# MLA keys squared and normalised out of PSUM, prompt queries left unnormalised until the exponential

## What is computed

```python
def rmsnorm(x, g):
    ms = jnp.mean(x32 * x32, axis=-1, keepdims=True)
    return (x32 * lax.rsqrt(ms + EPS)).astype(x.dtype) * g

def mla_keys(lat, kr, p):
    kv = (lat @ p["w_ukv"]).reshape(B, K, MLA_HEADS, MLA_NOPE + MLA_V)
    k_nope, v = kv[..., :MLA_NOPE], kv[..., MLA_NOPE:]
    k_rope = jnp.broadcast_to(kr[:, :, None, :], (B, K, MLA_HEADS, MLA_ROPE))
    k = rmsnorm(jnp.concatenate([k_nope, k_rope], axis=-1), p["g_qk_k"])
    return k, v

q = (rmsnorm(c_q, p["g_q_lora"]) @ p["w_uq"]).reshape(B, L, MLA_HEADS, MLA_QK)
q = jnp.concatenate([q[..., :MLA_NOPE], rope(q[..., MLA_NOPE:], pos)], axis=-1)
q = rmsnorm(q, p["g_qk_q"])
s = jnp.einsum('bqhd,bkhd->bhqk', q, k) * (MLA_QK ** -0.5)
w = jax.nn.softmax(jnp.where(mask, s, -jnp.inf), axis=-1)
```

## Time and profile before

| | before |
|---|---|
| median of 3 runs | 1527.66 us (1523.3 to 1532.15) |
| the profiled execution, its time | 1524.81 us |
| its span in the trace | 1523.0 us |
| PE busy | 1399.7 us (92%) |
| DVE busy | 785.7 us (52%) |
| ACT busy | 623.0 us (41%) |
| mean granted PE clock | 0.96 of full |

### The profile page before, as it was taken

One profiled execution on the slowest core, in us unless ns is written; L12 is line 12 of the kernel. 1 busy time (PEld: TensorE's weight loads), 2 busy tenths in 40 slices (PEclk: granted clock), 3 DMA queues, 4 the chain that ended last, 5 costly groups with the idle time before them and its releaser, 6 DMA issues.

```text
span 1523.0 us, 21364 instructions
## 1 busy us (share of the span) xinstructions
PE 1399.7 (92%) x8622; PEld 1135.2 (75%) x8622; DVE 785.7 (52%) x1140; ACT 623.0 (41%) x966; POOL 94.2 (6%) x80
## 2 busy tenths in 40 slices
PE   5998999999999989999479999999999999899991
PEld 5995667799999756777279847668999987567770
DVE  4336546533435347887353284464433344578763
ACT  4317634422224134565243285343222232355540
POOL 0300000000000011000203000000000000110002
PEclk9999999899999999999779999999999999899996
DMA  7223300033125457998722103000333163599955
GB/s 263 70 66 105 111 1 1 1 111 103 43 77 211 161 224 262 410 411 306 240 90 70 61 2 110 0 1 19 94 110 103 44 227 132 203 365 415 414 187 204
DMA packets 95927, 229.51 MB, mean 151 GB/s; under 512 B 14410, under 2 KB 64612, under 8 KB 82916
## 3 DMA queue, kind: packets, MB, share of 16 engines
q1 hardware_dynamic: 83252, 179.58, 32.6%
q0 software_dynamic: 7360, 29.89, 5.6%
q10 hardware_dynamic: 5232, 18.88, 3.1%
HBM read 197.69 MB, written 34.84 MB: 153 GB/s over the span
## 4 chain that ended last, share of the span: by engine, by line
PE 85%; DVE 4%; DMA 4%; ACT 3%; issue 2%; POOL 1%; ACTq 0%; POOLq 0%; SPq 0%; DVEq 0%
PE ps L763 10%; PE ps L765 10%; PE ps L764 10%; PE ps L1214 7%; PE ps L1194 3%; PE ps L1192 3%; PE ps L1193 3%; PE ps L1035 3%; PE ps L1100 2%; PE ps L789 2%; PE ps L1102 2%; PE ps L1101 2%; PE ps L791 2%; PE ps L790 2%; DMA rows_back<-xrow_d,row_of 2%
## 5 line engine op out<-in xcount | busy, mean ns | idle before, releaser
L1670 DVE TENSOR_TENSOR work<-work,ps 128x544 f32<-128x544 f32 x48 | 34.6, 721 | 211.2 <-ACT work L1525 211.2
L1525 ACT ACTIVATE work<-ps 128x544 f32<-128x544 f32 x48 | 30.0, 625 | 247.4 <-PE ps L765 247.4
L764 PE MATMUL ps<-xn_r,ksv_r 128*128 128x272 f32 x384 | 112.1, 292 | 0.0
L708 POOL DMA_INDIRECT rows_back<-xrow_d,row_of x32 | 38.1, 1192 | 1192.2 <-DVE row_of L2011 976.1
L764 PE MATMUL ps<-xn_r,work_r 128*128 128x272 f32 x384 | 110.7, 288 | 0.0
L1194 PE MATMUL ps<-ew_r,rows_tok_r 128*128 128x512 f32 x256 | 100.1, 391 | 0.0
L790 PE MATMUL ps<-wr_r,qt_ht_r 128*128 128x256 f32 (+1 forms) x320 | 93.1, 291 | 0.0
L789 PE MATMUL ps<-work_r,qt_ht_r 128*128 128x256 f32 x240 | 72.4, 302 | 14.0 <-DVE rows_lo_r L1670 7.9
L1670 DVE TENSOR_TENSOR ew_r<-ew,gu_hi_a_r 128x2048 fp32r<-128x2048 f32 x32 | 73.1, 2290 | 17.1 <-ACT gu_hi_a_r L1546 17.1
L764 PEld LDWEIGHTS ps<-xn_r,ksv_r 128*128 128x128 f32 x384 | 73.7, 192 | 0.0
L764 PEld LDWEIGHTS ps<-xn_r,work_r 128*128 128x128 f32 x384 | 72.1, 188 | 0.0
(11 more groups left out here) (348 smaller groups left out, 4066.9 us busy)
## 6 DMA issues: line engine op xcount, KB each, us to landing
wr<-in_w_in SPq DMA_DIRECT2D x68, 512.0 KB, 4.7
ew<-in_w_exp_gate SPq DMA_DIRECT2D x32, 1024.0 KB, 6.6
ew<-in_w_exp_up SPq DMA_DIRECT2D x32, 1024.0 KB, 10.2
ew<-in_w_exp_down SPq DMA_DIRECT2D x32, 1024.0 KB
wr<-in_w_out SPq DMA_DIRECT2D x16, 512.0 KB, 4.1
rows_d<-yo_a ACTq DMA_DIRECT2D x16, 512.0 KB
rows_d<-yo_b ACTq DMA_DIRECT2D x16, 512.0 KB
xres_d<-x_keep SPq DMA_DIRECT2D x2, 2048.0 KB, 7.0
```

The source lines that it names most:

```text
L764: mm(out_[h], w_hi, x_lo[:, c], start=False, stop=False, skip_group_check=True)
L1670: return v_.tensor_tensor(o_, a, b, op)
```

## The change

- **Keys.** ACT no longer copies the key part to SBUF; it squares the 512 key columns straight out of PSUM. DVE adds 64 squares a head (not 96), copies the values, and writes the normalised tile with two multiplications, one of the rotated key by the factor (256 columns) and one of the key part out of PSUM (512). The copies L1414 and L1793, the 768-column square and the 768-column multiplication of a key tile are gone. The rotated key's own sum of squares is made once a layer by three DVE operations ahead of the stage (`kr_ss`, `kr_bias`), and comes in as the bias of the logarithm.
- **Queries.** The sample tile is now first (`Q_ORDER`), and is normalised as before. The four prompt tiles are not multiplied: their sums go to `q_rs`, which one logarithm and one exponential turn into factors after `softplus_tail(1)`. In the scores, the exponential takes the factor as its scale, and a new DVE operation multiplies the negated maximum (128x1) by it, behind the maximum itself. ACT now squares a query out of PSUM right after its copy.
- **Banks and order.** Products use three pairs of banks (0 to 5) and run three tiles ahead for n up to 9; all transposes use banks 6-7, so transposes(n) wait for `kq_evac(n-1)`. `busy(4, 2)` is gone.

```diff
+Q_ORDER = [4, 0, 1, 2, 3]
...
+        kr_ss, kr_bias = small[:, 72:79], small[:, 80:87]
+        q_rs = small[:, 96:128].rearrange("p (t h) -> p t h", t=4)
...
-                    b = 2 * (n % 2)
-                    if n >= 2:
-                        pe.wait_ge(kq_raw[0], at(kq_raw, l, n - 1))
+                    b = 2 * (n % 3)
+                    if 3 <= n < 10:
+                        pe.wait_ge(kq_n[0], at(kq_n, l, n - 2))
+                    if n >= 10:
+                        pe.wait_ge(kq_sq[0], at(kq_sq, l, n - 2))
...
-                kq_products(0)
-                kq_products(1)
+                for n in range(3):
+                    kq_products(n)
                 for n in range(12):
-                    if n < 10:
-                        kq_products(n + 2)
-                    m = KM[n] if n < 7 else TM[n - 7]
+                    if 7 <= n < 9:
+                        kq_products(n + 3)
+                    m = KM[n] if n < 7 else TM[Q_ORDER[n - 7]]
                     if n == 11:
-                        pe.wait_ge(kq_raw[0], at(kq_raw, l, 12))
+                        pe.wait_ge(kq_sq[0], at(kq_sq, l, 12))
                         z_products(0)
-                    if n >= 2:
-                        pe.wait_ge(kq_ev[0], at(kq_ev, l, n - 1))
-                    if n == 10:
-                        busy(4, 2)
-                    pe.wait_ge(kq_n[0], at(kq_n, l, n + 1))
+                    if n:
+                        pe.wait_ge(kq_ev[0], at(kq_ev, l, n))
+                    if n < 8:
+                        pe.wait_ge(kq_n[0], at(kq_n, l, n + 1))
+                    else:
+                        pe.wait_ge(kq_raw[0], at(kq_raw, l, n - 6))
                     if m < P:
                         stand(pe)
                     for h in range(HEADS):
-                        ins = nc.tensor.transpose(bank(4 + 2 * (n % 2) + h // 4, m, QK, P * (h % 4)),
+                        ins = nc.tensor.transpose(bank(6 + h // 4, m, QK, P * (h % 4)),
                                                   kw[0:m, n % 3, QK * h:QK * h + QK], ident[0:m, 0:m])
                     ins.then_inc(kq_tp[0], 1)
+                    if n < 7:
+                        kq_products(n + 3)
...
-                    f(kss[0:m, n % 2], kss[0:m, n % 2], ACT.Ln, bias=eps[0:m], scale=1.0 / QK).then_inc(kq_ln[0], 1)
+                    f(kss[0:m, n % 2], kss[0:m, n % 2], ACT.Ln, bias=kr_bias[0:m, n:n + 1] if n < 7 else eps[0:m], scale=1.0 / QK).then_inc(kq_ln[0], 1)
...
+                    b = 2 * (n % 3)
                     act.wait_ge(kq_mm[0], at(kq_mm, l, n + 1))
-                    if n >= 3:
+                    if n >= 2:
+                        act.wait_ge(kq_ss[0], at(kq_ss, l, n - 1))
+                    if n < 7:
+                        f(sq[0:m, n % 2, 0:HEADS * NOPE].rearrange("p (h n) -> p h n", h=HEADS),
+                          ps[0:m, b:b + 2, :].rearrange("p b (h n) -> p (b h) n", h=4)[:, :, 0:NOPE], ACT.Square).then_inc(kq_sq[0], 1)
+                        if n >= 2:
+                            kq_evac(n - 2)
+                        kq_rstd(n)
+                    else:
                         act.wait_ge(kq_tp[0], at(kq_tp, l, n - 2))
-                    if n < 7:
-                        f(kw[0:m, n % 3, :].rearrange("p (h n) -> p h n", h=HEADS)[:, :, 0:NOPE],
-                          ps[0:m, b:b + 2, :].rearrange("p b (h n) -> p (b h) n", h=4)[:, :, 0:NOPE], ACT.Copy).then_inc(kq_cp[0], 1)
-                    else:
                         f(kw[0:m, n % 3, :].rearrange("p (b n) -> p b n", b=2), ps[0:m, b:b + 2, 0:384], ACT.Copy).then_inc(kq_cp[0], 1)
-                    if n:
-                        kq_rstd(n - 1)
-                    if n >= 2:
+                        f(sq[0:m, n % 2, :].rearrange("p (b n) -> p b n", b=2), ps[0:m, b:b + 2, 0:384], ACT.Square).then_inc(kq_sq[0], 1)
+                        if n == 8:
+                            kq_rstd(7)
                         kq_evac(n - 2)
-                    act.wait_ge(kq_raw[0], at(kq_raw, l, n + 1))
...
+                act.wait_ge(kq_ss[0], at(kq_ss, l, 12))
+                f(q_rs, q_rs, ACT.Ln, bias=eps, scale=1.0 / QK).then_inc(kq_ln[0], 1)
+                act.wait_ge(kq_ln[0], at(kq_ln, l, 9))
+                f(q_rs, q_rs, ACT.Exp, scale=-0.5).then_inc(kq_rs[0], 1)
...
-                    f(pr[0:m, n % 3, 0:nk], ps[0:m, n % 3, 0:nk], ACT.Exp, bias=nmax[0:m, n % 3:n % 3 + 1],
+                    f(pr[0:m, n % 3, 0:nk], ps[0:m, n % 3, 0:nk], ACT.Exp, bias=nmax[0:m, n % 3:n % 3 + 1], scale=q_rs[:, t, h:h + 1] if t < 4 else 1.0,
...
+                kr_sq = rope_t.rearrange("p a n -> p (a n)")[:, 0:NKT * ROPE].rearrange("p (t n) -> p t n", t=NKT)
+                link(tt(kr_sq, krt[:, :, :], krt[:, :, :], ALU.mult))
+                link(v_.tensor_reduce(kr_ss, kr_sq, AX, ALU.add))
+                link(v_.tensor_scalar(kr_bias, kr_ss, 1.0 / QK, EPS, ALU.mult, ALU.add))
...
-                        v_.tensor_copy(vv[0:m, n, :].rearrange("p (h n) -> p h n", h=HEADS),
-                                       ps[0:m, b:b + 2, :].rearrange("p b (h n) -> p (b h) n", h=4)[:, :, NOPE:P])
-                        v_.tensor_copy(k3[0:m, :, NOPE:QK], krt[0:m, n, :].unsqueeze(1).to_broadcast([m, HEADS, ROPE])).then_inc(kq_raw[0], 1)
+                        rs = kss[0:m, n % 2].unsqueeze(2)
+                        kv = ps[0:m, b:b + 2, :].rearrange("p b (h n) -> p (b h) n", h=4)
+                        dve.wait_ge(kq_sq[0], at(kq_sq, l, n + 1))
+                        v_.tensor_reduce(kss[0:m, n % 2], sq[0:m, n % 2, 0:HEADS * NOPE].rearrange("p (h n) -> p h n", h=HEADS), AX, ALU.add).then_inc(kq_ss[0], 1)
+                        v_.tensor_copy(vv[0:m, n, :].rearrange("p (h n) -> p h n", h=HEADS), kv[:, :, NOPE:P])
+                        dve.wait_ge(kq_rs[0], at(kq_rs, l, n + 1))
+                        if n >= 3:
+                            dve.wait_ge(kq_tp[0], at(kq_tp, l, n - 2))
+                        tt(k3[0:m, :, NOPE:QK], krt[0:m, n, :].unsqueeze(1).to_broadcast([m, HEADS, ROPE]), rs.to_broadcast([m, HEADS, ROPE]), ALU.mult)
+                        tt(k3[0:m, :, 0:NOPE], kv[:, :, 0:NOPE], rs.to_broadcast([m, HEADS, NOPE]), ALU.mult).then_inc(kq_n[0], 1)
                     else:
...
-                    if n:
-                        kq_scale(n - 1)
-                    dve.wait_ge(kq_sq[0], at(kq_sq, l, n + 1))
-                    v_.tensor_reduce(kss[0:m, n % 2], sq[0:m, n % 2, :].rearrange("p (h n) -> p h n", h=HEADS), AX, ALU.add).then_inc(kq_ss[0], 1)
-                kq_scale(11)
+                        if n == 8:
+                            kq_scale(7)
+                        dve.wait_ge(kq_sq[0], at(kq_sq, l, n + 1))
+                        v_.tensor_reduce(kss[0:m, n % 2] if t == 4 else q_rs[:, t, :], sq[0:m, n % 2, :].rearrange("p (h n) -> p h n", h=HEADS), AX, ALU.add).then_inc(kq_ss[0], 1)
...
-                    v_.tensor_reduce(nmax[0:m, n % 3:n % 3 + 1], ps[0:m, n % 3, 0:nk], AX, ALU.max, negate=True).then_inc(s_max[0], 1)
+                    low_ = nmax[0:m, n % 3:n % 3 + 1]
+                    ins = v_.tensor_reduce(low_, ps[0:m, n % 3, 0:nk], AX, ALU.max, negate=True)
+                    if t < 4:
+                        link(ins)
+                        h = n % HEADS
+                        ins = tt(low_, low_, q_rs[:, t, h:h + 1], ALU.mult)
+                    ins.then_inc(s_max[0], 1)
```

More of the change, by code:

```diff
@@ L71 @@
 DVE_FILLS = 12
-DVE_LINKS = 53
+DVE_LINKS = 88
 def at(sem_per, layer, n):
@@ L343, in hybrid_streaming_encoder @@
         kq_mm = sem("kq_mm", 12)
-        kq_cp = sem("kq_cp", 12)
-        kq_raw = sem("kq_raw", 12)
+        kq_cp = sem("kq_cp", NTILE)
+        kq_raw = sem("kq_raw", NTILE)
         kq_sq = sem("kq_sq", 12)
         kq_ss = sem("kq_ss", 12)
-        kq_ln = sem("kq_ln", 12)
-        kq_rs = sem("kq_rs", 12)
-        kq_n = sem("kq_n", 12)
+        kq_ln = sem("kq_ln", 9)
+        kq_rs = sem("kq_rs", 9)
+        kq_n = sem("kq_n", 8)
         kq_tp = sem("kq_tp", 12)
@@ L878, in kq_products @@
                     else:
-                        t, m = n - 7, TM[n - 7]
+                        t, m = Q_ORDER[n - 7], TM[Q_ORDER[n - 7]]
                         if n == 7:
@@ L1400, in kq_evac @@
                     else:
-                        dst, m, gain = qT[0:QK, :, TO[n - 7]:TO[n - 7] + TM[n - 7]], TM[n - 7], gains[0:QK, G_Q:G_Q + 1]
-                    b = 4 + 2 * (n % 2)
+                        dst, m, gain = qT[0:QK, :, TO[Q_ORDER[n - 7]]:TO[Q_ORDER[n - 7]] + TM[Q_ORDER[n - 7]]], TM[Q_ORDER[n - 7]], gains[0:QK, G_Q:G_Q + 1]
+                    b = 6
                     f(dst, ps[0:QK, b:b + 2, :].rearrange("p b (h n) -> p (b h) n", h=4)[:, :, 0:m], ACT.Copy, scale=gain).then_inc(kq_ev[0], 1)
@@ L1774, in kq_scale @@
                 def kq_scale(n):
-                    m = KM[n] if n < 7 else TM[n - 7]
```

(17 more changed lines are left out.)

6 lines of the change are left out of this document (1 added, 5 removed).

## The result

The changed kernel takes 1543.18 us (median of 20 executions, 1531.62 to 1553.42). The kernel before, run beside it as often, takes 1531.79 us (one of its twenty, at 4807.57 us, stands apart, and nothing here explains it). The ratio is 1.0084, 95% interval 1.0060 to 1.0107: slower by 0.84%, some 12 us. The forecast was 1524.2 us and its range ended at 1532. The profiled execution took 1533.97 us, span 1532.2, mean granted clock 0.952 (before: 1524.81, 1523.0 and 0.96).

The account below looks back on a forecast made before the run. The PE was taken as the bound (85% of the chain), with ACT and DVE mattering only where it waits. 1527.66 - 8.4 (stage) + 1.4 (scores) + 3.5 (clock) = 1524.2 us, range 1517 to 1532.

Parts of the forecast that it names:

- Key tiles, start, tail, together 4.2 us a layer: Keys' and queries' stage: key tiles become PE-bound at 2.65 us, `z_products(0)` starts at 37.4 not 41.65; 8.4 us in all.
- The prices by shape: Keys' stage: new ACT and DVE work priced by profile rows of the same shape, 2.21 and 2.48 us a key tile.
- the 128x256 product that no row had: Key tiles on DVE: the 256-column multiplication, between half of 0.69 and 0.69, taken at 0.42 us.
- Scores, 0.7 us a layer: Scores: the 128x1 multiplication, 0.2 us a unit, mostly fits DVE's idle time; 1.4 us in all, bounds 0 and 12.8.
- Scale of the exponential, nothing: Scores on ACT: the exponential's scale replaces a constant and costs nothing.
- The clock, +3.5 once: Ahead of `z_products(0)`: PE clock may fall, +0.1 to +5.5 us a layer, 3.5 taken; about even chances each layer, counted once.
- The base of 1527.66 us: Whole kernel before: the time from which the forecast starts; three runs before scatter by 4 us to both sides.
- Both fall: Rival, ahead of `z_products(0)`: the clock falls early in both layers, 1527.7 us; chance 0.20.
- The scores get slower: Rival, scores: multiplication delays the exponential and PE, outweighing the stage's gain above 0.13 us a unit; 1532 us; chance 0.10.
- The rule weighed against the row: Ahead of `z_products(0)`: by the skill page transposes don't count, both layers fall; against it, an earlier transposes-only row kept clock 1.00.

Follow-up runs that it names:

- e1: Changed kernel plus one unread 512-column matmul ahead of transposes(9) and one ahead of transposes(10) in the keys' stage; 1534.8 us.
- e9: e1 plus unread products ahead of each `values` in the fourth score tile only (t = 0, eight units); 1520.38 us.
- e3: Changed kernel without the multiplication of the negated maximum and without the exponential's scale; 1530.0 us.
- e2: Kernel before with only the score part added, the multiplication of the maximum and the exponential's scale, both by ones; 1545.8 us.
- e12: Changed kernel timed once more, unchanged, beside the kernel before; 1544.3 us, ratio interval 0.9971 to 1.0062.
- e5: e1 and e3 together: changed kernel with the unread matmuls in the keys' stage, without multiplication and scale in the scores; 1525.69 us.
- e6: e1 plus unread products ahead of each `values` in two score tiles, those of 128 keys and of 32 rows; 1527.4 us.
- e10: e1 plus two unread products a layer (128 and 256 columns) in two waits of the fourth score tile; 1522.7 us.
- e11: Kernel before plus two unread products a layer (128 and 256 columns) in the fourth score tile; 1524.44 us.
- e8: Kernel before with the multiplication of the negated maximum by ones in the first four score tiles, no scale on the exponential; 1535.3 us.

## Why the prediction was wrong

- **Key tiles, start, tail, together 4.2 us a layer: right, measured 3.9.** 2.6 to 2.8 us a tile, two waits of 1.20 and 1.32, `z_products(0)` at 37.7 against a forecast of 37.4. With the clock held (e1, e9) the scores start at 88.4 instead of 92.3 to 92.8. The prices by shape held too: the 128x256 product that no row had was taken at 0.42 and takes 0.425 us, mean of twelve.
- **Scores, 0.7 us a layer: right as work.** First scores to last `turn_out`, with the clock high to the last 3 us, take 72.3 us without the multiplication (e3) and 73.2 with it: 0.9 a layer. By the bases it is 0.4 (e2) to 0.9 (e3).
- **Scale of the exponential, nothing: right for the time, wrong as a duration.** It costs 0.09 us each (below); that this is nothing in time stands on the base of e2, which holds it and the multiplication and rose by 0.8 us in all.
- **The clock, +3.5 once: this is the step that failed, in size and in place.** It looked at one place, ahead of `z_products(0)`, and bounded it at 5.5 us a layer with even chances. There the fall came in four of the six profiled layers of the changed keys' stage without e1's matmuls (one of two, both of e3, one of e12), and cost 6.8 us (in all four the scores start at 95.0 to 95.2, against 88.4), over the upper bound. The bound doubled `z_products(0)` and `z_products(1)` and nothing else. The low stretch lasted 20.5 us, and the transposes ahead of each (1.94 and 1.92 us for about 1.07) and the two unread matmuls (3.76 for 1.98) took twice as long too. The second place was in no term: the fourth tile of the scores, where a fall costs about 11 us. By the lumps in its times the kernel before already had it in some executions, and the score part of the change made it likelier. Together the low time rose from 139 to 172 us, 0.36 x 33 = 12 us, where the forecast had 3.5.
- **The base of 1527.66 us** came from three executions. Over 99, the kernel before has a mean of 1533.0. The three lay at 1523, 1528 and 1532, which fits the two lower lumps (their clocks are not known); it was read as scatter, and put on the range alone.
- **The sum over again, by the means.** The changed kernel has 1541.6 where the forecast was 1524.2, 17.4 more: 5.3 by the base of the kernel before, 3.7 by a gain of 3.3 in the work instead of 7.0, and 8.5 by the clock (12 instead of 3.5). The clock is the largest of the three.
- **The rivals.** "Both fall" was nearest in kind, at 1527.7. "The scores get slower" had the place but another mechanism: it wanted 0.13 us a unit to reach the PE by way of ACT; what reached it was the clock.
- **The rule weighed against the row.** Behind transposes and two waits the clock fell in four of six layers, and with full matmuls between them in none of ten (e1, e5, e6, e9, e10). The Trainium skill (TensorE: Matmul & The Clock Gate, Part 4: PE-mode transpose) says that a transpose doesn't count as PE-busy in the same way. Read as not at all, as the prediction did, it would have had both layers fall every time: nearer to this than the even chances taken from the earlier trace rows, but the two layers that held speak against it as an absolute, and since e1's matmuls filled the waits as well, the runs don't part the two.

Two things stay open. Stages and scores alone should make the base 7 us shorter by the forecast (6 by the two measured pieces, 2 x 3.9 less 2 x 0.9), and it is 3.3 to 4 us shorter (e9 and e11 differ by 4.1 in the median too). In the profiles, the keys start 1.1 us later on average in the kernels with the changed stage (122.1 for 121.0), and 0.9 us more lies behind the last scores, in code that is the same; why wasn't tried. And whether the multiplication or the scale makes the fall in the fourth tile likelier, e8 doesn't tell.

## What to carry to other kernels

Where TensorE is the bound, read how close each thin stage is to losing its clock before pricing an edit in nanoseconds: here edits that moved the base by less than 2 us moved the time by 8 to 10. Write down time and mean clock of every execution; a straight line through them parts the work from the clock, and showed here, from twenty executions, a gain of 3 us in the work that the medians hid. A stage shortened around a wait should get its unread matmuls put back into the new waits (e1, free), and a stage of thin units that falls in some executions may be worth them in every unit (e9). Each place has to be tried by itself: the same products cost 0.6 us in the fourth tile and 7.5 in the last (e9, e6), and why they differ wasn't looked into.

## What the runs showed of the hardware

- The exponential with a scale for each partition takes longer than with a constant: 563 ns for 472 at 128x256, 455 for 365 at 128x128, each the mean of 16. Groups of ACT by form, before and changed:

```profile
L1479 ACT ACTIVATE work<-ps,nmax 128x256 f32<-128x256 f32 x16 | 7.6, 472 | 10.5 <-DVE nmax L1847 10.5
```

```profile
L1491 ACT ACTIVATE work<-ps,nmax,small 128x256 f32<-128x256 f32 x16 | 9.0, 563 | 9.6 <-DVE nmax L1682 9.6
```

- The clock stays low through a stage in which the PE is busy nearly all the time: 38.99 of 41.00 us, at 0.50 (the second row of e12 above). From 267 to 299.2 these are matmuls of 32 to 288 columns, busy 30.99 of 32.20 us; then come two of 512 columns, the last small transposes and, from 302.6, the 272-column products of the next stage, and at 308.0 the clock is back.
- Whether it falls differs between executions of one kernel: the changed one had the long fall in one layer of its first profile and in both of its second, and the times of the kernel before lie in three lumps, 11 us apart.
